# A layer norm in finer pieces between a convolution and its output projection, with TensorE kept going in the waits

## The reference

```python
ab = h @ w_in + b_in
a, b = split(ab, 2)
u = a * sigmoid(b)
u = causal_depthwise_conv(u, dw, width=31) + dw_b     # 1024 channels
u = (u - mean(u)) * rsqrt(var(u) + 1e-6) * ln_g + ln_b  # over the 1024 features of a token
u = silu(u)
x = x + u @ w_out + b_out
```

## Time and profile before

| | |
|---|---|
| median of 3 runs | 999.09 us (998.18 to 999.73) |
| profiled execution | 998.9 us, span of its instructions 996.9 us |
| TensorE matmul busy | 965.1 us, 97% of the span |
| TensorE weight load busy | 797.6 us, 80% |
| VectorE busy | 779.0 us, 78% |
| ScalarE busy | 479.0 us, 48% |
| GpSimd busy | 44.1 us, 4% |
| mean granted TensorE clock | 0.991 |

### The profile page before, as it was taken

One profiled execution on the slowest core, in us unless ns is written; L12 is line 12 of the kernel. 1 busy time (PEld: TensorE's weight loads), 2 busy tenths in 40 slices (PEclk: granted clock), 3 DMA queues, 4 the chain that ended last, 5 costly groups with the idle time before them and its releaser, 6 DMA issues.

```text
span 996.9 us, 13078 instructions
## 1 busy us (share of the span) xinstructions
PE 965.1 (97%) x4504; PEld 797.6 (80%) x4504; DVE 779.0 (78%) x1463; ACT 479.0 (48%) x727; POOL 44.1 (4%) x64
## 2 busy tenths in 40 slices
PE   4999999999988999999999999999999899999998
PEld 3788888888977888888888888888877678888887
DVE  4897887776958787878788878786767689787873
ACT  5553544565233644435455435355767665353531
POOL 0100000010210200000000000000203000000000
PEclk9999999999989999999999999999999999999999
DMA  9966555573837457474656474645643135746431
GB/s 329 317 212 211 182 197 205 183 241 118 265 108 252 135 188 236 147 246 155 228 183 204 149 246 142 237 159 179 213 167 127 43 127 180 243 151 227 163 132 43
DMA packets 128445, 186.16 MB, mean 187 GB/s; under 512 B 5936, under 2 KB 104368, under 8 KB 128400
## 3 DMA queue, kind: packets, MB, share of 16 engines
q1 hardware_dynamic: 123744, 169.89, 50.1%
q0 software_dynamic: 4368, 14.96, 4.6%
q10 hardware_dynamic: 288, 0.72, 0.2%
HBM read 184.50 MB, written 1.05 MB: 186 GB/s over the span
## 4 chain that ended last, share of the span: by engine, by line
PE 87%; DVE 5%; DMA 3%; ACT 2%; issue 1%; POOL 1%; SPq 1%; DVEq 0%; ACTq 0%
PE pg L440 16%; PE pg L446 16%; PE pg L444 16%; PE acc L440 11%; PE acc L444 11%; PE acc L446 11%; PE acc L612 4%; DMA raw<-in_ffn_w_in 3%; DVE w_lo L1150 2%; PE pt L517 1%; POOL mix L406 1%; ACT w_hi L814 1%; SPq L324 1%; DVE mix L1425 1%; ACT mix L964 0%
## 5 line engine op out<-in xcount | busy, mean ns | idle before, releaser
L1150 DVE TENSOR_TENSOR w_lo<-raw,w_hi 128x1024 fp32r<-128x1024 f32 x320 | 374.2, 1221 | 29.2 <-ACT w_hi L814 27.9
L814 ACT CAST w_hi<-raw 128x1024 fp32r<-128x1024 f32 x320 | 315.8, 1046 | 23.5 <-DMA raw<-in_ffn_w_in 22.8
L440 PE MATMUL pg<-w_hi,a_hi 128*128 128x512 f32 x720 | 281.6, 391 | 0.0
L446 PE MATMUL pg<-w_hi,a_lo 128*128 128x512 f32 x720 | 280.5, 390 | 0.0
L444 PE MATMUL pg<-w_lo,a_hi 128*128 128x512 f32 x720 | 280.5, 390 | 0.0
L1239 DVE STREAM_TRANSPOSE mix<-hs 32x128 f32<-32x128 f32 x640 | 193.8, 303 | 9.6
L446 PEld LDWEIGHTS pg<-w_hi,a_lo 128*128 128x128 f32 x720 | 135.2, 188 | 28.2
L440 PEld LDWEIGHTS pg<-w_hi,a_hi 128*128 128x128 f32 x720 | 135.4, 188 | 27.9 <-issue 0.4
L444 PEld LDWEIGHTS pg<-w_lo,a_hi 128*128 128x128 f32 x720 | 135.3, 188 | 27.6
L1231 DVE SCALAR_TENSOR_TENSOR hs<-pg,rstd,hs 128x256 f32<-128x256 f32 x80 | 38.3, 483 | 99.4 <-ACT hs L859 99.4
L859 ACT ACTIVATE hs<-pg,rstd 128x256 f32<-128x256 f32 x80 | 37.9, 475 | 159.7 <-PE pg L446 159.7
(11 more groups left out here) (122 smaller groups left out, 619.8 us busy)
## 6 DMA issues: line engine op xcount, KB each, us to landing
raw<-in_ffn_w_in SPq DMA_DIRECT2D x176, 512.0 KB, 5.0
raw<-in_ffn_w_out SPq DMA_DIRECT2D x88, 512.0 KB, 5.7
raw<-in_attn_w_qkv SPq DMA_DIRECT2D x24, 512.0 KB, 4.7
diags<-in_conv_diags POOLq DMA_DIRECT2D x20, 512.0 KB, 4.7
raw<-in_conv_w_in SPq DMA_DIRECT2D x16, 512.0 KB, 5.4
raw<-in_conv_w_out SPq DMA_DIRECT2D x8, 512.0 KB, 4.2
raw<-in_attn_w_out SPq DMA_DIRECT2D x8, 512.0 KB, 3.8
gain<-in_ffn_norm POOLq DMA_DIRECT2D x3, 512.0 KB, 4.9
```

The lines of the kernel that those rows point to most:

```text
L440: mm = pe.matmul(dst[j], stat_hi, m_hi, start=first, stop=False)
L446: mm = pe.matmul(dst[j], stat_lo, m_hi, start=False, stop=last)
L814: nc.scalar.copy(w_hi[n % RING][:, cols], raw[n % RAW][:, cols]).then_inc(hi_done, 1)
L1150: nc.vector.tensor_tensor(w_lo[n % RING][:, cols], raw[n % RAW][:, cols], w_hi[n % RING][:, cols].bitcast(F32), ALU.subtract).then_inc(lo_ ...
```

## The change

- TensorE turns tiles 0, 1 and 2 and groups 0 and 1 before the last group's taps, `taps(9)`, not after them; groups 7, 8 and 9 follow the taps.
- The normalisation is done in four parts of 256 features: VectorE does parts 0, 2 and 3 (part 3 after the remainders of tiles 0 and 1), ScalarE does part 1. Each part has its own semaphore.
- The transposes back (`norm_back(j)`, pair j) write tiles 0 and 1 to acc banks 0 and 2, the others to pg bank 1 and to pt. Pairs 0 and 1 are turned before the projection, pair 2 before the fourth piece of unit 0, pair 3 before the second piece of unit 1.
- Silu, rounding and remainder go tile by tile, eight of each; the projection's pieces wait for the tile that they need.
- TensorE runs 13 matmuls of 512 columns before `norm_back(0)` and 3 before the projection, on a unit of weights that is already there, into acc bank 1, whose first projection matmul overwrites what they leave.

```diff
--- before.py
+++ after.py
@@ -253,7 +253,7 @@
         tap_done = sem("tap_done")
         c_turned = sem("c_turned")
         ln_b_set = sem("ln_b_set")
-        ln_done = [sem(f"ln_done{t}") for t in range(TT)]
+        ln_done = [sem(f"ln_done{j}") for j in range(KT // 2)]
         n_turned = sem("n_turned")
         act_done = sem("act_done")
         s_hi_done = sem("s_hi_done")
@@ -291,6 +291,12 @@
 
             return (pg, pt)[j // 2][:, j % 2, :].rearrange("p (i n) -> p i n", i=2)
 
+        def norm_turn(kt):
+
+            if kt < 2:
+                return acc[:, 2 * kt, 0:T]
+            return (pg[:, 1, :], pt[:, 0, :], pt[:, 1, :])[kt // 2 - 1][:, kt % 2 * T:(kt % 2 + 1) * T]
+
         def w_in_source(s):
 
             kind, layer, which, _ = STAGES[s]
@@ -644,25 +650,45 @@
                 turn_group(5).then_inc(c_turned, 1)
                 taps(8)
                 turn_group(6)
+                turn_tile(0)
+                turn_tile(1).then_inc(c_turned, 1)
+                turn_group(0)
+                turn_group(1)
+                turn_tile(2).then_inc(c_turned, 1)
                 taps(9)
                 turn_group(7)
-                for g in (0, 1):
-                    turn_group(g)
-                turn_tile(0)
-                turn_tile(1).then_inc(c_turned, 1)
-                turn_tile(2).then_inc(c_turned, 1)
                 turn_group(8)
                 turn_group(9).then_inc(c_turned, 1)
-                for j in range(KT // 2):
-                    pe.wait_ge(ln_done[j // 2], 2)
-                    for i in range(2):
-                        for k in range(2):
-                            mm = pe.transpose((pg, pt)[j // 2][:, j % 2, k * T + i * P:k * T + (i + 1) * P],
+
+                def norm_back(j):
+
+                    pe.wait_ge(ln_done[j], 2)
+                    for k in range(2):
+                        for i in range(2):
+                            mm = pe.transpose(norm_turn(2 * j + k)[:, i * P:(i + 1) * P],
                                               xg[:, i, (2 * j + k) * P:(2 * j + k + 1) * P], ident)
                     mm.then_inc(n_turned, 1)
-                for w in range(KT // 2):
-                    pe.wait_ge(s_lo_done, w + 1)
-                    second_unit(s, u + 2 * chunks + w, a_left(w), w == 0, w == KT // 2 - 1)
+
+                def keep_warm(count):
+                    spare = w_hi[(u + 2 * chunks) % RING]
+                    for _ in range(count):
+                        pe.matmul(acc[:, 1, :], spare[:, 0:P], spare[:, 0:BANK], start=True, stop=True)
+
+                unit_ready(u + 2 * chunks)
+                keep_warm(13)
+                norm_back(0)
+                norm_back(1)
+                keep_warm(3)
+                for w in range(KT // 2 - 1):
+                    hooks = {0: lambda w=w: pe.wait_ge(s_lo_done, 2 * w + 1), 2: lambda w=w: pe.wait_ge(s_lo_done, 2 * w + 2)}
+                    if w == 0:
+                        hooks[1] = lambda: pe.wait_ge(act_done, 2)
+                        hooks[3] = lambda: norm_back(2)
+                    if w == 1:
+                        hooks[1] = lambda: norm_back(3)
+                    second_unit(s, u + 2 * chunks + w, a_left(w), w == 0, False, hooks)
+                pe.wait_ge(s_lo_done, KT)
+                second_unit(s, u + 2 * chunks + KT // 2 - 1, a_left(KT // 2 - 1), False, True)
 
             def attn(s):
                 u = UNIT0[s]
@@ -954,19 +980,20 @@
                 act.wait_ge(power_done, POWER_AT["ln", 0, 0] + 1)
                 act.wait_ge(ln_b_set, 1)
                 for i in range(2):
-                    nc.scalar.activation(xg[:, i, BANK:2 * BANK].rearrange("p (b n) -> p b n", b=2),
-                                         pt[:, :, i * T:(i + 1) * T], ACT.Identity,
+                    nc.scalar.activation(xg[:, i, T:2 * T], by_parity(1)[:, i, :], ACT.Identity,
                                          bias=ln_b[:, i:i + 1], scale=ln_r[:, i:i + 1]).then_inc(ln_done[1], 1)
-                for j in range(KT // 2):
-                    act.wait_ge(n_turned, j + 1)
-                    for k in range(2):
-                        kt = 2 * j + k
-                        mm = nc.scalar.activation(cv[:, kt, :].rearrange("p (m i) -> p i m", i=2),
-                                                  (pg, pt)[j // 2][:, j % 2, k * T:(k + 1) * T].rearrange("p (i m) -> p i m", i=2),
-                                                  ACT.Silu, bias=chan[:, kt, W + 2:W + 3], scale=chan[:, kt, W + 1:W + 2])
-                    mm.then_inc(act_done, 1)
-                    act.wait_ge(act_done, j + 1)
-                    nc.scalar.copy(a_hi[:, 2 * j:2 * j + 2, :], cv[:, 2 * j:2 * j + 2, :]).then_inc(s_hi_done, 1)
+
+                def silu(kt):
+                    if kt % 2 == 0:
+                        act.wait_ge(n_turned, kt // 2 + 1)
+                    nc.scalar.activation(cv[:, kt, :].rearrange("p (m i) -> p i m", i=2),
+                                         norm_turn(kt).rearrange("p (i m) -> p i m", i=2),
+                                         ACT.Silu, bias=chan[:, kt, W + 2:W + 3], scale=chan[:, kt, W + 1:W + 2]).then_inc(act_done, 1)
+                    act.wait_ge(act_done, kt + 1)
+                    nc.scalar.copy(a_hi[:, kt, :], cv[:, kt, :]).then_inc(s_hi_done, 1)
+
+                for kt in range(KT):
+                    silu(kt)
                 tick(u + 2 * chunks)
                 for w in range(1, 4):
                     tick(u + 2 * chunks + w)
@@ -1338,10 +1365,14 @@
                     tap(2, j)
                 assert tapped[:VK] == TAPS_DONE
 
+                def stats(j):
+                    for i in range(2):
+                        mm = nc.vector.bn_stats(bn[:, i, j, :], by_parity(j)[:, i, :])
+                    return mm
+
                 for n, j in enumerate((2, 0, 1, 3)):
                     dve.wait_ge(c_turned, n + 1)
-                    for i in range(2):
-                        mm = nc.vector.bn_stats(bn[:, i, j, :], by_parity(j)[:, i, :])
+                    mm = stats(j)
                 link(mm)
                 for i in range(2):
                     mm = nc.vector.bn_aggr(mv[:, i, :], bn[:, i, :, :])
@@ -1351,14 +1382,23 @@
 
                 nc.vector.scalar_tensor_tensor(out=ln_b, in0=mv[:, :, 0], scalar=-1.0, in1=ln_r,
                                                op0=ALU.mult, op1=ALU.mult).then_inc(ln_b_set, 1)
-                for i in range(2):
-                    nc.vector.tensor_scalar(xg[:, i, 0:BANK].rearrange("p (b n) -> p b n", b=2),
-                                            pg[:, :, i * T:(i + 1) * T], mv[:, i, 0:1], ln_r[:, i:i + 1],
-                                            ALU.subtract, ALU.mult).then_inc(ln_done[0], 1)
-                for j in range(KT // 2):
-                    dve.wait_ge(s_hi_done, j + 1)
-                    nc.vector.tensor_tensor(a_lo[:, 2 * j:2 * j + 2, :], cv[:, 2 * j:2 * j + 2, :],
-                                            a_hi[:, 2 * j:2 * j + 2, :].bitcast(F32), ALU.subtract).then_inc(s_lo_done, 1)
+                def norm(j):
+                    for i in range(2):
+                        nc.vector.tensor_scalar(xg[:, i, j * T:(j + 1) * T], by_parity(j)[:, i, :], mv[:, i, 0:1],
+                                                ln_r[:, i:i + 1], ALU.subtract, ALU.mult).then_inc(ln_done[j], 1)
+
+                def rest(kt):
+                    dve.wait_ge(s_hi_done, kt + 1)
+                    nc.vector.tensor_tensor(a_lo[:, kt, :], cv[:, kt, :], a_hi[:, kt, :].bitcast(F32),
+                                            ALU.subtract).then_inc(s_lo_done, 1)
+
+                norm(0)
+                norm(2)
+                rest(0)
+                rest(1)
+                norm(3)
+                for kt in range(2, KT):
+                    rest(kt)
                 tick(u + 6)
                 tick(u + 7)
                 dve.wait_ge(b_out_loaded, 16)
```

## The result

| | before | changed |
|---|---|---|
| median of 6 runs | 999.21 us (997.49 to 999.73) | 1003.56 us (1002.82 to 1005.23) |
| profiled execution, span | 998.9, 996.9 us | 1004.43, 1002.6 us |
| TensorE matmul busy | 965.1 us | 969.3 us |
| mean granted TensorE clock | 0.991 | 0.990 |

The changed kernel is slower: ratio 1.0045, 95% interval 1.0032 to 1.0057, 4.35 us between the medians. The forecast was 1002.8 with a range of 1000.4 to 1004.8.

The account below looks back on a forecast made before the run. TensorE holds 87% of the span, but VectorE's w_lo, transfers and update hold the boundary before the next stage. 998.9 + 3.04 + 0.7 = 1002.6, median 0.2 higher: 1002.8 us, range 1000.4 to 1004.8.

Parts of the forecast that it names:

- The first four steps: Turns moved, norm in pieces of 256, warming, first tile: projection begins at 294.02 instead of 296.51, 2.5 us sooner.
- The back-turns in the units: norm_back(2) and norm_back(3) inside units 0 and 1 hold up ScalarE's last tiles; VectorE's w_lo block starts 3.04 us later.
- Nothing makes them shorter: SP's weight transfers are each issued 3.04 us later, and the last still takes about 7.2 us.
- The clock term: At the next stage's first turn: 4.8 us at half clock, 1.4 more, costing 0.7 us; bounds nothing and 0.8.
- The stop: TensorE stands idle before the next stage's first turn, 7.3 us instead of 2.74.
- Rival B: Boundary not held by VectorE's w_lo; the last unit's matmuls set the end, 1.5 us sooner: 997.6 us; 7%.
- Rival C: Clock falls before the projection, 1.85 us lost ahead of norm_back(3): 1004.6 us; 10%.
- Rival D: ScalarE's tiles cost 0.7 instead of 0.9, transfers land sooner; 1 us of delay left: 1000.1 us; 7%.
- the shift: The 3.04 us delay of VectorE's w_lo block, passed on through transfers and casts to the update and next stage's turn.

Follow-up runs that it names:

- e1: Changed kernel with VectorE's w_lo of units u+10 and u+11 moved out of the block into its waits before the layer norm; 997.66 us.
- e7: Changed kernel with one w_lo pair (u+10) moved into VectorE's wait between the remainders of tiles 3 and 4; 1000.32 us.
- e3: Changed kernel with all four back-turns ahead of the projection and norm(3) ahead of rest(0), w_lo block left in place; 999.28 us.
- e9: The changed kernel itself, unaltered, measured again in the third set; 1004.09 us, ratio 1.0047 to the kernel before.
- e11: Kernel before with 15 warming matmuls in TensorE's 4.78 us wait, nothing else; 998.51 us.
- e4: Changed kernel without its sixteen warming matmuls; 1006.47 us.
- e12: Changed kernel with all back-turns ahead of the projection, w_lo of u+10 and u+11 before the norm, and no warming matmuls; 993.20 us.
- e2: Kernel before with the w_lo pairs of u+10 and u+11 moved into VectorE's wait before the layer norm; 995.80 us.

## Why the prediction was right

Its steps against the profile, the changed kernel's times less 1.59 us (the distance between the two times of group 8's bias), so that they stand in the time of the kernel before:

| step | predicted | measured |
|---|---|---|
| bn_stats of part 3 | 288.55 | 288.61 |
| first normalising instruction | 290.83 | 290.91 |
| norm_back(0) | 291.87 | 291.96 |
| silu of tile 0 | 292.52 | 292.65 |
| projection begins | 294.02 | 294.29 |
| norm_back(2), norm_back(3) | 298.10, 301.26 | 298.48, 301.69 |
| silu of tile 6 | 301.91 | 302.33 |
| last a_lo ends | 304.27 | 304.74 |
| w_lo block begins | 304.19 (+3.04) | 304.65 (+3.50) |
| first transfer issued | 306.6 | 307.03 |
| update | 322.10 (+3.04) | 322.22 (+3.16) |
| turn at the boundary | 323.56 | 323.69 |
| stop ahead of it | 7.3 | 6.78 |
| clock at the boundary | +0.7 | +1.14 |
| all | +3.7 | +4.31 |

*The first four steps* (turns moved, norm in pieces, warming, first tile) hold to 0.13 us, from durations of 512 and 1024 columns alone: an L1387 pair takes 0.99, as worked out (0.98), and a cast of 256 takes 0.41. The warming matmuls cost nothing: thirteen of them end 0.42 us before norm_back(0).

*The back-turns in the units* were priced at 3.04 and came to 3.50. Of the 0.46, 0.27 are in the projection's start: 0.14 us pass between the remainder and the first matmul, where I had put 0.05, silu of tile 0 is 0.13 late, and 0.05 are lost in that tile's silu and cast. Another 0.16 lie in TensorE's five pieces up to norm_back(3), where the first pair of matmuls after a wait or a transpose takes longer than the others (0.70 against 0.62). The term was mis-sized by a sixth. The mechanism is what the runs show: e1 and e7 leave TensorE's program alone, e3 puts the same work in another order, and they move the end by 6.6, 4.4 and 4.5 us of stretch.

*"Nothing makes them shorter"*, of the transfers, was a little wrong. From the start of the w_lo block to the update it is 17.57 us instead of 17.91; the last transfer takes 6.86 instead of 7.19. That took back 0.34 of the 0.46, so that the update is only 0.12 off is in part luck: two errors of opposite sign. I had argued it from one row. e7 gives reason to doubt it further: with one pair out of the block the update gains 3.23 where the moved instructions are worth 2.3.

*The clock term* was the one that failed in size, 1.14 for 0.7 and beyond its own bound of 0.8. It is the difference of 16.91 and 15.77, and the clock's alone only if VectorE's pace costs the same in both, which no run separates. I took the time from TensorE's return to the rise of the clock to be 4.8 us, as at 292.89 in the kernel before; it was 5.9. In e9, the same kernel again, it was 5.3, and the difference 0.85. The other profiles show too that this time is no constant: 4.5 in the kernel before, 4.2 in e7 and 5.8 in e11 at the same place, 8.4 after the norm in e4. The bound should have been drawn from more stretches than two.

*The stop* was forecast at 7.3 us and was 6.78, though the turn came 0.13 later than forecast: TensorE's own path ended 0.7 later than the 316.2 I had for it, 0.46 of that since unit 2 waits for the same late w_lo block. It costs nothing, as this path didn't end last.

*A row misread.* The prediction has eight transposes back from 292.89. There are sixteen, in two rows, the second of which it left out:

```profile
294.65 1.91 PE L660 MATMUL pt<-consts,xg 128*128 128x128 f32 x8
```

So transposes fill the first 3.6 of the 4.8 us that the clock took to rise there, twice as many as the prediction says. No term of the sum hangs on it.

*Rival B* (the boundary isn't held by VectorE): the update has no idle time before it in the changed kernel, and comes 3.16 later. It fell. *Rival C* (the clock falls before the projection): the clock stood at 1.00 in every slice from 286 to 296, so this one fell too. The Trainium skill (TensorE: Matmul & The Clock Gate, Part 4) would have transposes not count as busy work; the clock stood at 1.00 through eight of them here, and in e12 through sixteen after 3.47 us of idleness, with no matmul between. The rows don't show the rule at work, and don't refute it either, for the clock doesn't fall at every gap. *Rival D* (the shift is taken up): a tile costs ScalarE 0.93 and not 0.7 (silu from 303.92 to the next at 304.85), and only 0.34 us came back on the transfers.

That the shift reaches the end in full, which the prediction took from TensorE's 87% share of the chain, is shown by what follows the stretch: 660.2 to 661.5 us in all fourteen profiles, while the stretch itself runs from 45.8 to 59.9.

## What to carry to other kernels

A wait that is split into finer pieces changes whose queue is behind it. Before an engine's wait is moved later, list what stands behind it in that engine's order, and follow that work to the next boundary: here six independent instructions behind eight small ones cost more than the whole head start of TensorE. Work that depends on nothing in the wait belongs into the wait: moving two such pairs gave 3.7 us in the kernel before. The changed kernel with its back-turns in front, worth nothing by itself, is 5.9 us faster than the kernel before once they are moved, without any engine working faster.

And when the holder of a boundary is removed, count the next one in full: e1 missed by 3.7 us as its chain had a second link, VectorE's own backlog, just behind the transfers.

## What the runs showed of the hardware

The granted clock does not answer to the length of the idle time alone. In the fourteen profiles it fell eleven times between the norm and the end of the stretch, 1.7 to 5.3 us after TensorE's last work. In four of these cases (the boundary of the kernel before, of e1 and of e7, and the norm of e2) TensorE was already at work again when it fell. The shortest gap followed by a fall was e1's at the boundary, 2.34 us; e12's gap of 3.47 us had none.

```profile
318.14 0.66 PE L523 MATMUL pt<-consts,xg 128*128 128x128 f32 x4 [2.34 <-DVE xg L1204]
```

```profile
318.00:319.00 1.00, 0.86 (x6) 0.98 0.87 298
319.00:320.00 1.00, 1.00 (x4) 0.50 1.09 376
```

It came back 3.8 (e2) to 8.4 us (e4) after work began again. What keeps it up is cheap: thirteen matmuls in a wait that ends later anyway took nothing, and without warming the changed kernel had a stretch 2.5 us longer.

The scatter of the runs (996.5 to 1002.6 us for the kernel before over three sets) is larger than most of the effects here. In the profiles, which are one run each, what follows group 8's bias repeats well and what lies ahead of it does not: part of that is in clock stretches of the first stage, part in single waits for a diagonal matrix of 0.2 to 1.9 us, which eight of the fourteen profiles have and six don't. Comparing a stretch between two fixed instructions resolved 0.3 us in single profiles (57.39 and 57.13, 55.18 and 55.16 in repeats) where the medians resolved one or two.
